# The gelu of the gating halves in a two-block transformer kernel, written out with square and tanh

## What is computed

```python
h = rmsnorm_2(x, norm_mix_w[l])
z = h @ w_in[l]
u, v, q, k_c, v_c, k_s, v_s, k_w, v_w, g_raw = jnp.split(z, offsets, axis=-1)
a = gmlp_group(u, v, ...)          # the gating half
b = nsa_group(q, k_c, v_c, ...)    # the attention half
mix = jnp.concatenate([rmsnorm_2(a, ...), rmsnorm_2(b, ...)], axis=-1)
x = x + mix @ w_o[l]

def gmlp_group(u, v, norm_w, ws, bs):
    u = jax.nn.gelu(u).reshape(B, nc, CHUNK, H_A, HEAD_DIM)
    v = rmsnorm_2(jax.nn.gelu(v), norm_w).reshape(B, nc, CHUNK, H_A, HEAD_DIM)
    w = jnp.where(causal[None], ws, 0).astype(v.dtype)
    sv = jnp.einsum('hts,bcshd->bcthd', w, v) + bs.T...
    return (u * sv).reshape(B, S, D_A)
```

## Time and profile before

| | |
|---|---|
| median of 3 runs | 2560.29 us |
| lowest and highest | 2559.78 and 2564.14 us |
| profiled execution, its own time | 2559.84 us |
| its span | 2557.7 us |
| mean granted TensorE clock | 0.996 of full |
| TensorE busy | 2518.2 us (98%) |
| VectorE busy | 1315.8 us (51%) |
| ScalarE busy | 566.9 us (22%) |
| GpSimd busy | 1519.2 us (59%) |
| second mixer's steps, about | 1938 to 2158 us of the span |

### The profile page before, as it was taken

One profiled execution on the slowest core, in us unless ns is written; L12 is line 12 of the kernel. 1 busy time (PEld: TensorE's weight loads), 2 busy tenths in 40 slices (PEclk: granted clock), 3 DMA queues, 4 the chain that ended last, 5 costly groups with the idle time before them and its releaser, 6 DMA issues.

```text
span 2557.7 us, 33017 instructions
## 1 busy us (share of the span) xinstructions
PE 2518.2 (98%) x11986; PEld 2058.2 (80%) x11986; DVE 1315.8 (51%) x1556; ACT 566.9 (22%) x1033; POOL 1519.2 (59%) x858
## 2 busy tenths in 40 slices
PE   8999999999999999999999999999999988999998
PEld 6888888778888888888888778888887776888887
DVE  5555527656555315556137656555226656655522
ACT  2110014652111001110015552111013564111000
POOL 5666666436666666666665536666664322666664
PEclk9999999999999999999999999999999999999999
DMA  4233222113222322332322112332233111332232
GB/s 166 96 98 98 94 96 75 58 42 98 93 96 98 99 93 97 98 95 93 99 96 69 56 50 93 98 121 93 98 99 132 57 35 34 99 96 93 99 99 74
DMA packets 66149, 228.67 MB, mean 89 GB/s; under 512 B 8721, under 2 KB 11665, under 8 KB 65681
## 3 DMA queue, kind: packets, MB, share of 16 engines
q1 hardware_dynamic: 64352, 225.67, 27.1%
q10 hardware_dynamic: 1712, 1.82, 0.2%
HBM read 225.36 MB, written 2.10 MB: 89 GB/s over the span
## 4 chain that ended last, share of the span: by engine, by line
PE 96%; DVE 2%; ACT 1%; POOL 1%; issue 1%; DMA 0%; SPq 0%; DVEq 0%; POOLq 0%; ACTq 0%
PE bank L606 28%; PE bank L608 28%; PE bank L607 28%; PE bank L623 2%; PE bank L755 2%; PE bank L740 2%; PE bank L724 1%; PE bank L629 1%; PE bank L725 1%; PE bank L978 1%; PE bank L993 1%; DMA raw<-in_stream 0%; POOL wl L570 0%; PE bank L614 0%; PE bank L970 0%
## 5 line engine op out<-in xcount | busy, mean ns | idle before, releaser
L570 POOL TENSOR_TENSOR wl<-raw,wh 128x1024 fp32r<-128x1024 f32 x412 | 1035.7, 2514 | 34.5
L567 POOL TENSOR_SCALAR wh<-raw 128x1024 fp32r<-128x1024 f32 x412 | 445.5, 1081 | 985.8 <-PE bank L608 947.8
L606 PE MATMUL bank<-xh,wh 128*128 128x512 f32 x2096 | 818.8, 391 | 0.2 <-POOL wl L570 0.2
L607 PE MATMUL bank<-xl,wh 128*128 128x512 f32 x2096 | 816.4, 389 | 0.0
L608 PE MATMUL bank<-xh,wl 128*128 128x512 f32 x2096 | 816.2, 389 | 0.0
L608 PEld LDWEIGHTS bank<-xh,wl 128*128 128x128 f32 x2096 | 393.5, 188 | 83.0
L607 PEld LDWEIGHTS bank<-xl,wh 128*128 128x128 f32 x2096 | 393.6, 188 | 81.4 <-issue 0.2
L606 PEld LDWEIGHTS bank<-xh,wh 128*128 128x128 f32 x2096 | 393.7, 188 | 81.1 <-POOL wl L570 0.6
L606 PE MATMUL bank<-acth,wh 128*128 128x512 f32 (+1 forms) x902 | 346.4, 384 | 0.0
L607 PE MATMUL bank<-actl,wh 128*128 128x512 f32 (+1 forms) x902 | 346.2, 384 | 0.0
L608 PE MATMUL bank<-acth,wl 128*128 128x512 f32 (+1 forms) x902 | 346.2, 384 | 0.0
(11 more groups left out here) (269 smaller groups left out, 2344.0 us busy)
## 6 DMA issues: line engine op xcount, KB each, us to landing
raw<-in_stream SPq DMA_DIRECT2D x412, 512.0 KB, 3.7
x<-in_x SPq DMA_DIRECT2D x4, 512.0 KB, 7.9
w1k<-in_w1k SPq DMA_DIRECT2D x1, 2048.0 KB, 9.0
w1v_low<-in_w1v SPq DMA_DIRECT2D x1, 1024.0 KB, 6.8
w1v_high<-in_w1v SPq DMA_DIRECT2D x1, 1024.0 KB, 10.0
out_dram<-x SPq DMA_DIRECT2D x4, 256.0 KB, 2.6
out_dram<-x SPq DMA_DIRECT2D x1, 768.0 KB, 3.7
invcount<-in_c_invcount ACTq DMA_DIRECT2D x1, 512.0 KB, 6.1
```

What stands on the lines that cost most here:

```text
L567: nc.gpsimd.tensor_scalar(wh[:, h, :, :], src, 1.0, 1.0, ALU.mult, ALU.mult)\
L570: nc.gpsimd.tensor_tensor(wl[:, h, :, :], src, wh[:, h, :, :].bitcast(F32), ALU.subtract).then_inc(split_done, 1)
L606: mm = nc.tensor.matmul(bank, wh[:, slot, k, :], rh, start=start, stop=False)
L607: mm = nc.tensor.matmul(bank, wh[:, slot, k, :], rl, start=False, stop=False)
```

## The change

The activation function Gelu_apprx_tanh is taken out for the eight gating tiles, and each gets five operations instead of two. With h = x/2, gelu(x) is h (1 + tanh(8 c r (h^2 + 1/(4c)) h)), c = 0.044715 and r = sqrt(2/pi):

1. `evacuate_half` (VectorE) takes the place of `evacuate2` in the same steps. It writes h = 0.5 bank rstd, in one instruction as before.
2. `gelu_square` (ScalarE) writes h^2 to a tile that is free at that time.
3. `gelu_inner` (VectorE, scalar_tensor_tensor with both tensors in SBUF) adds 1/(4c) and multiplies by h.
4. `gelu_tanh` (ScalarE), in place.
5. `gelu_outer` (VectorE, scalar_tensor_tensor, both in SBUF) adds 1 and multiplies by h, into the tile's place.

The tiles 0 to 3 are v and 4 to 7 are u. The free tile of v's tile n is `gu(n)`, and that of u's tile n is `gv[:, n - 4, :]`, which is why the squares 4 to 7 also wait for the last turn of v (`gated3`). The steps are written as tables of G, one for each operation. TensorE's, GpSimd's and SyncE's programs are not touched, `FILL2` is as it was, and the compressed MLP keeps its own gelu at step 8.

```diff
--- before.py
+++ after.py
+GELU_CUBE = 0.044715
+GELU_ROOT = (2 / np.pi) ** 0.5
+        gelu_sq = sem("gelu_sq")
+        gelu_in = sem("gelu_in")
+        gelu_th = sem("gelu_th")
         mean2 = sem("mean2")
         root2 = sem("root2")
         ss2_done = sem("ss2_done")
@@ -1352,9 +1357,17 @@
                 nc.scalar.activation((pta if i >= 2 else ptb)[:, a, 0:n], B[(3, 4)[G % 2]][:, 0:n], ACT.Copy)\
                     .then_inc(pte2_done, 1)
 
-            def gelu(n, unit, buf):
-                act.wait_ge(evac2, EVACUATED[unit])
-                nc.scalar.activation(buf, buf, ACT.Gelu_apprx_tanh).then_inc(gelu_done, 1)
+            def gelu_square(n):
+                act.wait_ge(evac2, EVACUATED[(GV_UNIT + GU_UNIT)[n]])
+                if n >= 4:
+                    act.wait_ge(shared_written, written("gated3"))
+                half, other = (gv[:, n, :], gu(n)) if n < 4 else (gu(n - 4), gv[:, n - 4, :])
+                nc.scalar.activation(other, half, ACT.Square).then_inc(gelu_sq, 1)
+
+            def gelu_tanh(n):
+                act.wait_ge(gelu_in, n + 1)
+                other = gu(n) if n < 4 else gv[:, n - 4, :]
+                nc.scalar.activation(other, other, ACT.Tanh, scale=8 * GELU_CUBE * GELU_ROOT).then_inc(gelu_th, 1)
 
...
@@ -1464,9 +1477,10 @@
                     high_q2(2)
                 if G in (31, 55):
                     compressed_copy(G // 32)
-                if G == 30:
-                    for t in range(4):
-                        gelu(t, GV_UNIT[t], gv[:, t, :])
+                if G in (17, 20, 23, 30, 37, 39, 40, 42):
+                    gelu_square((17, 20, 23, 30, 37, 39, 40, 42).index(G))
+                if G in (19, 22, 25, 31, 39, 41, 42, 43):
+                    gelu_tanh((19, 22, 25, 31, 39, 41, 42, 43).index(G))
                 if 34 <= G < 38:
                     token_squares(G - 34)
                 if G == 38:
@@ -1479,9 +1493,6 @@
                         scale_gated(c)
                 if G == 41:
                     square_b(1)
-                if G == 42:
-                    for t in range(4):
-                        gelu(4 + t, GU_UNIT[t], gu(t))
                 if G == 46:
                     high_q2(3)
                 if G in (46, 47):
@@ -1862,6 +1873,20 @@
                     dve.wait_ge(q2_low, 2 * pair)
                 evacuate2(Q_UNIT[pair], qall[:, :])
                 dve.wait_ge(evac2, EVACUATED[Q_UNIT[pair]])
+
+            def evacuate_half(n, dst):
+                dve.wait_ge(unit_used, u0 + n + 3)
+                V.scalar_tensor_tensor(dst, B[(n - 5) % 2][:, :], 0.5, rstd[:, :], ALU.mult, ALU.mult).then_inc(evac2, 1)
+
+            def gelu_inner(n):
+                dve.wait_ge(gelu_sq, n + 1)
+                half, other = (gv[:, n, :], gu(n)) if n < 4 else (gu(n - 4), gv[:, n - 4, :])
+                V.scalar_tensor_tensor(other, other, 1 / (4 * GELU_CUBE), half, ALU.add, ALU.mult).then_inc(gelu_in, 1)
+
+            def gelu_outer(n):
+                dve.wait_ge(gelu_th, n + 1)
+                half, other = (gv[:, n, :], gu(n)) if n < 4 else (gu(n - 4), gv[:, n - 4, :])
+                V.scalar_tensor_tensor(half, other, 1.0, half, ALU.add, ALU.mult).then_inc(gelu_done, 1)
 
             def shift2(which):
 
@@ -2093,19 +2118,19 @@
                     compressed_keys()
                 if G == 16:
                     dve.wait_ge(shared_written, written("hidden"))
-                    evacuate2(GV_UNIT[0], gv[:, 0, :])
+                    evacuate_half(GV_UNIT[0], gv[:, 0, :])
                 if G == 17:
                     compressed_values()
                 if G in (17, 18, 20, 21, 24, 26, 30, 31):
                     residual((17, 18, 20, 21, 24, 26, 30, 31).index(G))
                 if G == 19:
-                    evacuate2(GV_UNIT[1], gv[:, 1, :])
+                    evacuate_half(GV_UNIT[1], gv[:, 1, :])
                 if G == 20:
                     V.tensor_tensor(wst[:, :, :], wst[:, :, :],
                                     causal[:, :].rearrange("p (a n) -> p a n", a=1).to_broadcast([P, 8, P]), ALU.mult)\
                         .then_inc(ws_done, 1)
                 if G == 22:
-                    evacuate2(GV_UNIT[2], gv[:, 2, :])
+                    evacuate_half(GV_UNIT[2], gv[:, 2, :])
                 if G in (23, 25, 45, 49):
                     compressed_bias((23, 25, 45, 49).index(G))
                 if G in (25, 49):
@@ -2113,11 +2138,15 @@
                 if G in (28, 51):
                     compressed_normalise(G // 32)
                 if G == 29:
-                    evacuate2(GV_UNIT[3], gv[:, 3, :])
+                    evacuate_half(GV_UNIT[3], gv[:, 3, :])
                 if G in (33, 40, 57, 63):
                     add_blocks((33, 40, 57, 63).index(G))
                 if G in (32, 35, 38, 41):
-                    evacuate2(GU_UNIT[(32, 35, 38, 41).index(G)], gu((32, 35, 38, 41).index(G)))
+                    evacuate_half(GU_UNIT[(32, 35, 38, 41).index(G)], gu((32, 35, 38, 41).index(G)))
+                if G in (18, 21, 24, 31, 38, 40, 41, 43):
+                    gelu_inner((18, 21, 24, 31, 38, 40, 41, 43).index(G))
+                if G in (20, 23, 26, 32, 41, 42, 43, 44):
+                    gelu_outer((20, 23, 26, 32, 41, 42, 43, 44).index(G))
                 if 34 <= G < 38:
                     gated_copy(G - 34)
                 if G == 38:
```

## The result

| | before | after |
|---|---|---|
| median of 5 runs each, on one chip | 2560.53 us (2559.78 to 2564.14) | 2572.4 us (2571.69 to 2573.73) |
| ratio of the times, 95% interval | | 1.0049 [1.0038, 1.006] |
| span of the profiled execution | 2557.7 us | 2569.6 us |
| mean granted clock of TensorE over the span | 0.996 | 0.993 |

What follows compares the result with a forecast made beforehand. TensorE, busy 98% of the span, was taken as the bound, so only its waits count. The terms -1.36 + 0.1 + 1.05 + 1.20 + 1.87 + 0.65 + 0.83 + 1.13 = +5.47 gave 2565.8 us, range 2561.5 to 2569.5.

Steps and rivals of the forecast that it cites:

- the early steps: Steps 18 to 32: VectorE's eight added operations delay TensorE's wait at step 30 by 0.1 us, bounds 0 and 1.5.
- the `ptc` copy: Step 32, line 935: TensorE's 1.36 us wait for ScalarE's copy goes, as over 4 us leave the queue ahead.
- steps 39 to 44: waits and clock: Operations ahead of the scalings, `spatial_out` and line 918 lengthen TensorE's waits by 5.60 us; half clock adds 1.13.
- from step 45 on: Behind line 918: nothing is added, and no slack takes the lateness back; 0 us.
- The gain: Only TensorE's wait before line 935 at step 32 can be won: 1.36 us.
- the rival that made ScalarE the bound: All four removed table loads lie on TensorE's path: 5.1 us gained, 2555.2 us; chance 0.05.
- Prices on ScalarE: A gelu, square or tanh takes 0.62 us, a further one behind another 0.53; a table load takes 1.28.
- Steps 41 and 42: Gelu operations ahead of `spatial_out` delay TensorE: 1.20 us before `spatial(1)`, 1.87 before `spatial(2)`, including VectorE's wait for a tanh.
- the 0.05 for ScalarE's signal: Step 42: time from the end of tanh 5 to VectorE's start, 0.05 us.
- new waits before step 30: Sign that the forecast is wrong: TensorE waiting anew before step 30; no size given.
- The clock: `spatial(1)` and its two turns run at half clock behind a 2.96 us wait: loss 1.13 us, bounds -1.7 and +3.4.
- The rival with more stretches at half clock and VectorE held by GpSimd: Two more slow stretches at steps 39 to 44 (3.4 us) and 1.5 from early steps: 2569.5 us; chance 0.15.

Runs made afterwards that it cites:

- dummy_stt: Kernel before, with one unread operation on two SBUF tensors added on VectorE at step 24; 2563.22 us, ratio 1.0011.
- early_moved: Kernel after, with only v's tanh, inner and outer operations moved to other steps, away from GpSimd's splitting; 2567.25 us, ratio 1.0032.
- v_only: Kernel before, with the five-operation gelu for the four v tiles alone, u keeping the old gelu; 2563.57 us, ratio 1.0011.
- scal_first: Kernel after, with ScalarE's squares and tanhs moved behind the four scalings within the step; 2570.72 us, ratio 1.004.
- u_only: Kernel before, with the five-operation gelu for the four u tiles alone, v keeping the old gelu; 2570.14 us, ratio 1.0036.

## Why the prediction was wrong in size, and which of its mechanisms held

Term by term, with the lateness of the table above:

| term | predicted | measured |
|---|---|---|
| the early steps | +0.1 (0 to 1.5) | +3.17 |
| the `ptc` copy | -1.36 | -1.44 |
| steps 39 to 44: waits and clock | +6.73 (5.60 and 1.13) | +7.55 (3.95 and 3.60) |
| from step 45 on (2.4 of it clock) | 0 | +3.2 |
| start of the span | 0 | -0.59 |
| sum | +5.47 | +11.9 |

**The gain** was right and of the size read. No load of ScalarE's tables that went away bought anything elsewhere: four are gone, and only the wait at `ptc` shortened, so the rival that made ScalarE the bound falls.

**Prices on ScalarE** held: square and tanh at 0.61 and 0.62, one every 0.52. The kernel after at step 39, from the load on:

```profile
2070.63 1.28 ACT L1453 ACT_TABLE_LOAD   x1
2071.93 0.51 ACT L1453 ACTIVATE sq<-sq,smin 128x256 f32<-128x256 f32 x1
...
2072.44 0.61 ACT L1365 ACTIVATE gv<-mixed 128x512 f32<-128x512 f32 x1
2072.96 0.61 ACT L1370 ACTIVATE gv<-gv 128x512 f32<-128x512 f32 x1
2073.48 2.55 ACT L1434 ACTIVATE gvtok<-gvtok,gss 128x512 f32<-128x512 f32 x4
```

Two operations ahead of the scalings, and the wait grew by 3.46 - 2.42 = 1.04 against the predicted 1.05. The load and the activation behind it are 0.02 us apart, so the drain that the Trainium skill adds to a load ("ScalarE: Activation LUTs", "What ACT_TABLE_LOAD costs") is not in these rows either: the 1.28 stands, the further 1.38 does not.

**Steps 41 and 42.** VectorE's rows of the kernel after:

```profile
2081.03 0.68 DVE L1884 SCALAR_TENSOR_TENSOR gv<-gv,mixed 128x512 f32<-128x512 f32 x1
2081.63 0.68 DVE L1889 SCALAR_TENSOR_TENSOR mixed<-gv,mixed 128x512 f32<-128x512 f32 x1
2082.23 0.74 DVE L2019 SCALAR_TENSOR_TENSOR svt<-bank,vec,bsb 128x512 f32<-128x512 f32 x1
...
2087.39 0.69 DVE L1889 SCALAR_TENSOR_TENSOR mixed<-gv,mixed 128x512 f32<-128x512 f32 x1 [1.01 <-ACT gv L1370]
2087.99 0.74 DVE L2019 SCALAR_TENSOR_TENSOR svt<-bank,vec,bsb 128x512 f32<-128x512 f32 x1
```

Inner and outer stand 0.60 apart ahead of `spatial_out(0)`, and the wait is 2.98 against the 2.96 worked out. At step 42 VectorE idles 1.01 us until tanh 5, as drawn. The wait before `spatial(2)` came out at 1.47 and not over 2: the work ahead of it ran at half clock and filled part of it. The sum of the stretch, 7.55 against 6.73, is near, but its parts are not: 3.95 of waits stand against 5.60, and 3.60 of clock against 1.13, and the two errors offset each other, which is luck. The order of the operations was right, as the reorderings show. Of the small terms, no row of the kernel before shows the 0.05 for ScalarE's signal; here tanh 5 ends at 2087.36 and VectorE starts at 2087.39.

**The early steps are the step that failed.** "line 1983 at step 28 waits until 2034.17 in any case and swallows a lateness up to 1.8": the first collision was seen and priced, it ended 0.55 after GpSimd's operation where it was drawn to end with it, and VectorE came to line 1897 1.46 us later in its span than in the kernel before (up to 1.6 was worked out). What was not looked at is what stands between it and line 1983 on VectorE's queue. Line 1897, in step 27, moved just far enough to meet GpSimd's next unit itself, and both of its operations have their two tensors in SBUF; 1.40 became 4.32. The upper bound of 1.5 took one collision, and there are several. So 0.1 was put where 3.17 was measured. The text had named new waits before step 30 as what would make it wrong, and they came, at step 22 and before step 30's scores. `dummy_stt` shows that the one operation of step 24 is enough for the chain, and `early_moved` that with the same operations of v in other steps it does not start.

**The clock is the second.** It was priced from one wait at one product, 1.13 us. It took about 2.4 us from step 45 on, where the forecast added nothing, and 3.6 at steps 39 to 44. The kernel before already ran about 10 us at half clock behind step 45, which the earlier trace rows leave out. The rival with more stretches at half clock and VectorE held by GpSimd, 2569.5, named both causes and came nearest; it was given 0.15. What stood against it spoke of GpSimd at steps 41 to 44, not at steps 24 and 28. Its sum also takes the 1.13 off before it adds the 3.4, though these were to be *more* stretches; left in, 1.13 gives 2570.6, still under the measured 2572.4. The reason given, that a wait longer than 2.42 brings half speed, falls with `v_only`, `scal_first` and `u_only`, where 1.09 follows 2.43, 2.42 and 3.46. For `spatial(1)` itself the forecast came true, and it ran at half clock in each of the four kernels with 2.38 to 2.98 us ahead of it (after, `scal_first`, `u_only`, `early_moved`), but the reason for it is not shown. What the runs support is weaker: the kernel with more and longer waits in this stretch also spends more time at 1.2 GHz (full-speed time lost in the whole span, which is span times one less the mean clock, is 2569.6 x 0.007 = 18 us after and 2557.7 x 0.004 = 10 before), and which product is hit changes with a shift of a microsecond. Why it fell at 2171.2 in the kernel after, behind a wait that both kernels have, stays open; no run here was made to set the clock apart.

## What to carry to other kernels

Cost an added operation by what it stands ahead of in its queue, and put it behind whatever the bound engine waits for within the same step: the same operations in another order were 7.9 us apart here (2572.4 and 2564.53), and with all three orders put right the whole loss was gone. Where VectorE and GpSimd both work on SBUF, follow a collision to the *next* one, past every operation in between, before calling it swallowed, and count all of GpSimd's operations, not the longest alone. And before a function is rewritten to spare an engine's queue, move the old one behind the operation that is waited for: here that one number gave the whole 1.4 us of the gain in the trace, which is too small to be told from nothing by the medians.

## What the runs showed of the hardware

A copy in fp32 from SBUF to SBUF waits for GpSimd's operation as one on two tensors does (2.62 us against 0.41 for the next), while a reciprocal of one tensor does not (0.20). What waited ended, after GpSimd's operation, by nearly its own length: 0.55 us for the 0.69 us operation (2023.65 and 2024.20), 0.28 for the copy (2024.12 and 2024.40), 0.03 for the eight elements (2024.01 and 2024.04). GpSimd's `wh` operation, which reads one tensor, holds VectorE like its subtraction, which reads two: 1.51 and 2.77 us for the two of line 1897, against 0.69 each. And full speed behind a 3.46 us wait of TensorE in one kernel, and half speed behind 1.79 in another, were both unexpected.
